# Page loads by pairs in the latent attention of a decoder layer, and low parts moved between GpSimd and VectorE

## Chip, cores and metric

The kernel runs on one core of one Trainium2 chip. The metric is the device time of one execution in microseconds; of several runs the median is given.

## The reference

One layer of a hybrid decoder is computed for 512 prompt tokens and for 8 sample sequences of 8 new tokens each: a first SwiGLU half-step, one input projection, a convolution branch, a latent attention branch, a gated merge, and a second SwiGLU half-step. All is float32. What matters here is the attention of the sample sequences over their paged cache of 2048 past tokens (16 pages of 128 tokens; a page holds 256 latent values and 32 rotary key values for each token):

```python
ckv = jnp.concatenate([cache_ckv_l[pages].reshape(past, KV_LORA), ckv_new], axis=0)
kpe = jnp.concatenate([cache_kpe_l[pages].reshape(past, QK_ROPE), kpe_new], axis=0)
k = build_keys(ckv, kpe, w_uk, k_head_norm)   # k_nope = w_uk c per head, joined with kpe, rms-normed per head
s = einsum('qhd,khd->hqk', q, k) * SCALE; s = where(mask, s, -inf)
p = softmax(s); o_lat = einsum('hqk,kc->qhc', p, ckv); o = einsum('qhc,chd->qhd', o_lat, w_uv)
```

## The kernel before

Five engines work side by side, each with its own written order, and they meet only at semaphores. SyncE issues the transfers. Float32 products are made from split operands: a value is rounded to a high part (ScalarE copies it to type fp32r), the low part is the rest (a subtraction), and a product is the sum of high x high, low x high and high x low.

Stages by time: first FFN to about 410 us, input projection and gates to about 600, prompt attention to about 705, sample sequences 705 to 1018, merge and output product to about 1170, second FFN to the end.

`sequences` runs the eight sample sequences s = 0 to 7 on each engine: s = 0 by itself, then a hardware loop with two sequences a turn for s = 1 to 4, then 5, 6 and 7 by themselves. SyncE has its own division: 0 and 1 written out, and a loop of three turns for 2 to 7. The buffer is b = s mod 2. A sequence has 16 pages, handled as 8 pairs (`pp`, PAIRS = 8) and as 4 groups of four (`g`). For one page t:

- The transposed latent page comes into `c_ring`, a ring of 8 pages (`load_ring`, L731). ScalarE makes the high part of a pair, `cT_hi` (`pages_hi`, L1300); VectorE the low part, `cT_lo` (`pages_lo`, L2466). Both have two buffers, for even and odd pairs.
- TensorE multiplies the page with keys and queries, 12 matmuls of 288 columns (L1861). ScalarE copies the scores out (L1345) and squares the keys (L1351), VectorE sums the squares for each head (L2646). TensorE waits for the squares of the page before last, ScalarE for the sums of the page before last.
- For every four pages `kpeT` (`load_kpe`, L742) gives the rotary part in one product (`kpe_scores`, L1825) behind page 3, 7, 11 and 15, and VectorE adds it (L2654).
- The page in its natural layout, `c_nat`, with two buffers of 16 pages (`load_rows`, L737), is needed a sequence later for the values. GpSimd squares its rotary part at the end of a sequence (`squares`, L964).

While s goes through its pages, the softmax and the values of r = s - 1 are woven in. The generators `soft_pe`, `soft_dve` and `soft_act` advance one step at each `next`. For r up to 5 (`stacked(s)`, s up to 6) the order is: VectorE forms `k_inv`, scales, takes the maxima and subtracts; ScalarE makes the exponentials at pages 8 and 9, twice: `p_two[.., 0, ..]` rounded and `s_buf` in full; GpSimd makes their low part in `p_two[.., 1, ..]` (`probabilities_low`, L945 and L947); ScalarE makes high parts `c_hi` of the pairs of `c_nat` (`pair_high`, L1332; four slots, EARLY_PAIRS = 4), GpSimd low parts in place (`split_pair`, L937); TensorE multiplies four pairs ahead of page 12 and four ahead of page 15 (L1781, L1782), and folds and transposes the result within page 15 (L1791, L1796). In sequence 7 the values of r = 6 are one plain product ahead of page 12 (L1802), which ends with `den_sum` from VectorE (L2540, L1808).

The page numbers lie in SBUF (`pages`). SyncE loads one into a register at L726, and each transfer takes its source address from such a register:

```python
def page_of(s, t):
    return sp.value_load(pages[0:1, ds(s * NP + t, 1)], min_val=0, max_val=pages_t.shape[0] - 1)
```

`load_pages` finds four page numbers for each group and issues with them four transfers to the ring, four to `kpeT` and four to `c_nat`. Behind the last sequence SyncE issues the first weights of the merge (`load_merge`, L618 and L619); ScalarE splits them within sequence 7 (`split_hi`, L461), behind pair 4 and ahead of the high part of pair 6.

Of the kernel before, what the change touches and what calls it, by code (L numbers as in the profile page):

```python
# [20 lines left out]
ds = bass.ds  # L21
# [72 lines left out]
def layer(nc, x_t, cols_in, pages_t, pages_in, pages_k, state_conv, page_table, w, const, out):  # L94

    ctx = ExitStack()
    with ctx:
# [213 lines left out]
        split_made = sem("split_made")  # L311
# [14 lines left out]
        nat_in = [[sem(f"nat_in{b}{g}") for g in range(NP // 4)] for b in range(2)]  # L326
        ring_in = [sem(f"ring_in{g}") for g in range(2)]
# [194 lines left out]
        SPLITS = PAIRS + 2  # L522
        HIGHS = PAIRS + 2
        LATE_AT = 11
# [9 lines left out]
        def pair_made(r, j):  # L534

            return r * SPLITS + (EARLY_PAIRS + 1 if j < EARLY_PAIRS else j + 3)
# [11 lines left out]
        PEB = 6  # L548

# [46 lines left out]
        def _(sp):  # L596
# [131 lines left out]
            def load_ring(g, found):  # L728

                for u, page in enumerate(found):  # L730
                    sp.dma_start(c_ring[:, (4 * g + u + RING // 2) % RING, :], pages_t[ds(page, 1), :, :].rearrange("a p c -> (a p) c"))\  # L731
                        .then_inc(ring_in[g % 2], 16)

            def load_rows(b, g, found):

                for u, page in enumerate(found):
                    sp.dma_start(c_nat[:, b, 4 * g + u, :], pages_in[ds(page, 1), :, :].rearrange("a p c -> (a p) c")).then_inc(nat_in[b][g], 16)  # L737

            def load_kpe(g, found):

                for u, page in enumerate(found):
                    sp.dma_start(kpeT[u * DR:(u + 1) * DR, g % 2, :], pages_k[ds(page, 1), :, :].rearrange("a d t -> (a d) t")).then_inc(kpe_in[g % 2], 16)  # L742

            def load_pages(s, b, used=None):

                for g in range(NP // 4):
                    found = [page_of(s, 4 * g + u) for u in range(4)]
                    sp.wait_ge(ct_lo, s * PAIRS + (2 * g - 2))
                    load_ring(g, found)
                    sp.wait_ge(pe_scored, s * (NP // 4) + (g - 1))  # L750
                    load_kpe(g, found)
                    if used is not None:
                        sp.wait_ge(pages_used, used + 2 * (g + 1))
                    load_rows(b, g, found)

            sp.wait_ge(rows_done, 2 * NT + PT_TILES)
            found = [page_of(0, u) for u in range(4)]
# [4 lines left out]
            for g in (1, 2):  # L762
                load_rows(0, g, [page_of(0, 4 * g + u) for u in range(4)])
# [2013 lines left out]
```

## Time and profile before

| | us |
|---|---|
| median of 3 runs (lowest, highest) | 1537.03 (1536.82, 1539.36) |
| the profiled execution | 1533.52 |
| its span in the trace | 1531.5 |
| TensorE busy | 1491.3 |
| VectorE busy | 1067.9 |
| ScalarE busy | 655.5 |
| GpSimd busy | 454.3 |

The span runs from the first to the last instruction of the trace. Busy times do not count register, branch and semaphore instructions or the issuing of transfers, so SyncE has no busy time in the page's table; its instructions show in its own timeline, as SPq. The chain of waits follows the last instruction back to whatever released each step.

### The profile page before, as it was taken

To read this page: it belongs to the slowest core of one execution; us is meant where nothing else is said; L and a number is where in the kernel's file an instruction comes from. 1 tells how busy PE (TensorE), PEld (TensorE's weight loads), DVE (VectorE), ACT (ScalarE), POOL (GpSimd) and SP (SyncE) were. 2 spreads that over 40 slices of the span, in tenths; PEclk is the share of its full clock that TensorE was granted. 3 is DMA by queue.
4 is the path that set the end of the run, shared out by engine and by line. 5 is a ranking of instruction groups with operands and counts; after the bars stand their busy time and mean duration, and the time that the engine had idled before them with its cause. 6 is when DMAs were issued, how large, how long until landed. Compare 5 with 4: busy or idle time off the path is not lost.

```text
span 1531.5 us, 31143 instructions
## 1 busy us (share of the span) xinstructions
PE 1491.3 (97%) x10771; PEld 1434.9 (94%) x10771; DVE 1067.9 (70%) x1738; ACT 655.5 (43%) x1215; POOL 454.3 (30%) x463
## 2 busy tenths in 40 slices
PE   8999999999999999999999888999999999999999
PEld 8999999999999999588888888888999999999999
DVE  7999898421269975865888788854759998985000
ACT  6444445322221242464666666642434444445111
POOL 4000002454465744320344333223551000005432
PEclk9999999999999999999999999999999999999999
DMA  6233234222333651003444443432222332332322
GB/s 176 70 103 103 82 97 116 78 83 75 82 83 100 83 116 47 13 4 99 129 127 129 124 125 111 128 106 72 83 83 56 109 97 85 106 92 81 91 77 82
DMA packets 245460, 141.69 MB, mean 93 GB/s; under 512 B 22705, under 2 KB 242290, under 8 KB 245362
## 3 DMA queue, kind: packets, MB, share of 16 engines
q1 hardware_dynamic: 244498, 139.97, 33.1%
q8 instruction: 54, 0.88, 0.2%
q10 hardware_dynamic: 864, 0.48, 0.1%
q14 instruction: 44, 0.36, 0.1%
HBM read 136.82 MB, written 3.58 MB: 92 GB/s over the span
## 4 chain that ended last, share of the span: by engine, by line
PE 52%; issue 24%; SPq 11%; POOL 7%; DVE 3%; ACT 1%; DMA 1%; POOLq 0%; DVEq 0%; ACTq 0%
PE ps L493 28%; PE ps L1522 14%; POOL w_lobuf L468 7%; SPq L726 3%; SPq L731 3%; SPq L742 3%; SPq L737 2%; PE ps L1861 2%; PE ps L1647 1%; PE ps L1701 1%; PE ps L1676 1%; PE ps L479 1%; PE ps L1691 1%; DMA w_rawbuf<-in_ffn_w_gu 1%; DVE cT_lo L2466 1%
## 5 line engine op out<-in xcount | busy, mean ns | idle before, releaser
L468 POOL TENSOR_TENSOR w_lobuf<-w_rawbuf,w_hibuf 128x256 fp32r<-128x256 f32 (+1 forms) x328 | 316.4, 996 | 801.4 <-ACT w_hibuf L461 801.3
L1522 PE MATMUL ps<-xs,w 128*128 128x288 f32 x3192 | 427.7, 296 | 0.8 <-DVE w L1984 0.8
L1522 PEld LDWEIGHTS ps<-xs,w 128*128 128x128 f32 x3192 | 426.8, 188 | 1.5 <-issue 1.5
L461 ACT ACTIVATE w_hibuf<-w_rawbuf 128x1024 fp32r<-128x1024 f32 (+1 forms) x89 | 104.4, 1173 | 353.3 <-PE ps L493 332.9
L2192 DVE SCALAR_TENSOR_TENSOR xT<-ps,xT 128x576 f32<-128x576 f32 x23 | 17.4, 756 | 202.4 <-PE ps L493 202.4
L1984 DVE TENSOR_TENSOR w<-w_raw,w 128x512 fp32r<-128x512 f32 x228 | 154.0, 690 | 0.3 <-ACT w L1029 0.2
L493 PE MATMUL ps<-a_hi,w_lobuf 128*128 128x288 f32 x682 | 147.5, 297 | 0.0
L493 PE MATMUL ps<-a_hi,w_hibuf 128*128 128x288 f32 x682 | 147.2, 296 | 0.0
L493 PE MATMUL ps<-x_hi,w_hibuf 128*128 128x288 f32 x656 | 142.2, 298 | 4.1 <-POOL w_lobuf L468 2.9
L493 PE MATMUL ps<-a_lo,w_hibuf 128*128 128x288 f32 x682 | 145.5, 294 | 0.0
L493 PE MATMUL ps<-x_lo,w_hibuf 128*128 128x288 f32 x656 | 140.8, 296 | 0.0
L493 PE MATMUL ps<-x_hi,w_lobuf 128*128 128x288 f32 x656 | 140.7, 296 | 0.0
L1029 ACT ACTIVATE w<-w_raw 128x512 fp32r<-128x512 f32 x228 | 132.2, 624 | 5.7 <-DVE w_raw L1978 2.4
L1861 PE MATMUL ps<-kq_hi,cT_hi 128*128 128x288 f32 x512 | 119.6, 316 | 14.7 <-DVE cT_lo L2466 9.3
L2215 DVE SCALAR_TENSOR_TENSOR y<-ext,cols,y 128x512 f32<-128x512 f32 x120 | 110.6, 922 | 4.1 <-DVE y L2215 1.4
L1861 PE MATMUL ps<-kq_hi,cT_lo 128*128 128x288 f32 x512 | 111.3, 299 | 0.0
L1861 PE MATMUL ps<-kq_lo,cT_hi 128*128 128x288 f32 x512 | 111.3, 299 | 0.0
L493 PEld LDWEIGHTS ps<-x_hi,w_hibuf 128*128 128x128 f32 x656 | 105.4, 188 | 5.8 <-POOL w_lobuf L468 4.1
L493 PEld LDWEIGHTS ps<-a_hi,w_hibuf 128*128 128x128 f32 x682 | 110.2, 189 | 0.0
L493 PEld LDWEIGHTS ps<-a_lo,w_hibuf 128*128 128x128 f32 x682 | 109.3, 188 | 0.0
L493 PEld LDWEIGHTS ps<-a_hi,w_lobuf 128*128 128x128 f32 x682 | 109.0, 188 | 0.0
L1861 PEld LDWEIGHTS ps<-kq_hi,cT_hi 128*128 128x128 f32 x512 | 84.1, 194 | 25.3 <-DVE cT_lo L2466 10.4
(335 smaller groups left out, 2602.6 us busy)
## 6 DMA issues: line engine op xcount, KB each, us to landing
w_raw<-in_ffn_w_gu SPq DMA_DIRECT2D x76, 256.0 KB, 2.9
up_rows<-in_ffn_w_gu SPq DMA_DIRECT2D x72, 256.0 KB, 3.2
c_nat<-in_pages_in SPq DMA_DIRECT2D x128, 144.0 KB, 2.2
c_ring<-in_pages_t SPq DMA_DIRECT2D x128, 128.0 KB, 2.1
w_rawbuf<-in_w_in SPq DMA_DIRECT2D x58, 256.0 KB, 3.2
w_rawbuf<-in_ffn_w_down SPq DMA_DIRECT2D x32, 384.0 KB, 4.0
w_rawbuf<-in_ffn_w_down SPq DMA_DIRECT2D x32, 320.0 KB, 3.4
w_rawbuf<-in_ffn_w_gu SPq DMA_DIRECT2D x24, 256.0 KB, 3.4
```

Source lines behind the costliest of these rows:

```text
L461: act.activation(w_hibuf[:, r % HIS, 0:size], w_rawbuf[:, r, 0:size], ACT.Copy).then_inc(w_hi_done, 1)
L468: ins = pool.tensor_tensor(w_lobuf[:, r, part], w_rawbuf[:, r, part], w_hibuf[:, r % HIS, part].bitcast(F32), ALU.subtract)
L493: mm = pe.matmul(ps[0:width, 2 * s + h, 0:HALF], a, b[:, k, h * HALF:(h + 1) * HALF], start=first and i == 0 and j == 0, stop=last and i = ...
L726: return sp.value_load(pages[0:1, ds(s * NP + t, 1)], min_val=0, max_val=pages_t.shape[0] - 1)
L731: sp.dma_start(c_ring[:, (4 * g + u + RING // 2) % RING, :], pages_t[ds(page, 1), :, :].rearrange("a p c -> (a p) c"))\
L737: sp.dma_start(c_nat[:, b, 4 * g + u, :], pages_in[ds(page, 1), :, :].rearrange("a p c -> (a p) c")).then_inc(nat_in[b][g], 16)
L742: sp.dma_start(kpeT[u * DR:(u + 1) * DR, g % 2, :], pages_k[ds(page, 1), :, :].rearrange("a d t -> (a d) t")).then_inc(kpe_in[g % 2], 16)
L1029: act.activation(w7[b][:, slot, 0, :], src, ACT.Copy).then_inc(w7_hi, 1)
L1522: mm = pe.matmul(ps[:, seven_bank(f, slot), 0:HALF], m, xs[:, slot, n, k, :], start=k == 0 and j == 0, stop=k == KH - 1 and j == 2)
L1861: mm = pe.matmul(ps[:, page_banks(t) + half, 0:KQ], a, m[:, half, cols], start=k == 0 and j == 0, stop=k == 1 and j == 2)
L1984: dve.tensor_tensor(w7[b][:, slot, 1, :], w7_raw[b][:, slot, 1, :], w7[b][:, slot, 0, :].bitcast(F32), ALU.subtract).then_inc(w7_lo, 1)
L2215: dve.scalar_tensor_tensor(dst, src, cw, dst, op0=ALU.mult, op1=ALU.add).then_inc(conv_p_step, 1)
```

## The change

- SyncE loads by pairs of pages. `load_pair` looks up two page numbers and issues two ring transfers, then looks up two page numbers for two transfers to `c_nat`: in the first half of a sequence those of the upper eight pages of the sequence before, in the second half those of its own lower eight. After each odd pair `load_kpe` looks up four numbers and issues four transfers to `kpeT`, two pairs or more behind the ring. The ring has one semaphore for each of its four pairs, and each `c_nat` buffer one for all of its 16 pages.
- `pages_lo` moves from VectorE to GpSimd, except in sequence 0.
- The low parts of the probabilities move from GpSimd to VectorE, ahead of pair 5, with a semaphore of their own, `p_low`.
- GpSimd's splits of the value pairs are interleaved with `pages_lo`.
- ScalarE makes the high parts of the last four value pairs from page 10 on, not 11. TensorE places four pairs of values ahead of page 11 and four within page 14; the fold comes ahead of the products of page 15. VectorE copies `o_lat` behind page 13 and inverts the denominator behind page 14.

```diff
-        split_made = sem("split_made")
+        split_made, p_low = sem("split_made"), sem("p_low")
...
-        nat_in = [[sem(f"nat_in{b}{g}") for g in range(NP // 4)] for b in range(2)]
-        ring_in = [sem(f"ring_in{g}") for g in range(2)]
+        nat_in = [sem(f"nat_in{b}") for b in range(2)]
+        ring_in = [sem(f"ring_in{j}") for j in range(RING // 2)]
...
-        SPLITS = PAIRS + 2
+        SPLITS = PAIRS
-        LATE_AT = 11
+        LATE_AT = 10
...
-            return r * SPLITS + (EARLY_PAIRS + 1 if j < EARLY_PAIRS else j + 3)
+            return r * SPLITS + (j + 1)
...
+        def pages_lo(eng, s, pp):
+            eng.wait_ge(ct_hi, s * PAIRS + (pp + 1))
+            eng.tensor_tensor(cT_lo[:, pp % 2, :], ring_pair(pp), cT_hi[:, pp % 2, :].bitcast(F32), ALU.subtract).then_inc(ct_lo, 1)
...
             def page_of(s, t):
                 return sp.value_load(pages[0:1, ds(s * NP + t, 1)], min_val=0, max_val=pages_t.shape[0] - 1)
-            def load_ring(g, found):
-                for u, page in enumerate(found):
-                    sp.dma_start(c_ring[:, (4 * g + u + RING // 2) % RING, :], pages_t[ds(page, 1), :, :].rearrange("a p c -> (a p) c"))\
-                        .then_inc(ring_in[g % 2], 16)
-            def load_rows(b, g, found):
-                for u, page in enumerate(found):
-                    sp.dma_start(c_nat[:, b, 4 * g + u, :], pages_in[ds(page, 1), :, :].rearrange("a p c -> (a p) c")).then_inc(nat_in[b][g], 16)
-            def load_kpe(g, found):
-                for u, page in enumerate(found):
-                    sp.dma_start(kpeT[u * DR:(u + 1) * DR, g % 2, :], pages_k[ds(page, 1), :, :].rearrange("a d t -> (a d) t")).then_inc(kpe_in[g % 2], 16)
-            def load_pages(s, b, used=None):
-                for g in range(NP // 4):
-                    found = [page_of(s, 4 * g + u) for u in range(4)]
-                    sp.wait_ge(ct_lo, s * PAIRS + (2 * g - 2))
-                    load_ring(g, found)
+            def found(s, t0, n):
+                return [page_of(s, t0 + u) for u in range(n)]
+            def load_ring(pp, two):
+                for u, page in enumerate(two):
+                    sp.dma_start(c_ring[:, (2 * pp + u + RING // 2) % RING, :], pages_t[ds(page, 1), :, :].rearrange("a p c -> (a p) c"))\
+                        .then_inc(ring_in[pp % (RING // 2)], 16)
+            def load_rows(b, pp, two):
+                for u, page in enumerate(two):
+                    sp.dma_start(c_nat[:, b, 2 * pp + u, :], pages_in[ds(page, 1), :, :].rearrange("a p c -> (a p) c")).then_inc(nat_in[b], 16)
+            def load_kpe(s, g):
+                four = found(s, 4 * g, 4)
+                if not (isinstance(s, int) and s == 0 and g < 2):
                     sp.wait_ge(pe_scored, s * (NP // 4) + (g - 1))
-                    load_kpe(g, found)
+                for u, page in enumerate(four):
+                    sp.dma_start(kpeT[u * DR:(u + 1) * DR, g % 2, :], pages_k[ds(page, 1), :, :].rearrange("a d t -> (a d) t"))\
+                        .then_inc(kpe_in[g % 2], 16)
+            def load_pair(s, b, pp, used=None):
+                two = found(s, 2 * pp, 2)
+                sp.wait_ge(ct_lo, s * PAIRS + (pp - 3))
+                load_ring(pp, two)
+                if pp >= PAIRS // 2:
+                    q = pp - PAIRS // 2
+                    two = found(s, 2 * q, 2)
                     if used is not None:
-                        sp.wait_ge(pages_used, used + 2 * (g + 1))
-                    load_rows(b, g, found)
+                        sp.wait_ge(pages_used, used + (q + 1))
+                    load_rows(b, q, two)
+                elif used is not None:
+                    q = pp + PAIRS // 2
+                    two = found(s - 1, 2 * q, 2)
+                    sp.wait_ge(pages_used, used + (q + 1 - PAIRS))
+                    load_rows(1 - b, q, two)
+                if pp % 2:
+                    load_kpe(s - 1 if pp == 1 else s, 3 if pp == 1 else (pp - 3) // 2)
             sp.wait_ge(rows_done, 2 * NT + PT_TILES)
-            found = [page_of(0, u) for u in range(4)]
-            load_ring(0, found)
-            load_kpe(0, found)
+            for pp in range(2):
+                load_ring(pp, found(0, 2 * pp, 2))
+            load_kpe(0, 0)
             sp.wait_ge(prep_q, 1)
-            load_rows(0, 0, found)
-            for g in (1, 2):
-                load_rows(0, g, [page_of(0, 4 * g + u) for u in range(4)])
+            for pp in range(6):
+                load_rows(0, pp, found(0, 2 * pp, 2))
             sp.wait_ge(prep_tr, 2)
             sp.wait_ge(uk_split, 1)
-            found = [page_of(0, 4 + u) for u in range(4)]
-            load_ring(1, found)
-            load_kpe(1, found)
-            load_rows(0, 3, [page_of(0, 12 + u) for u in range(4)])
-            for g in (2, 3):
-                found = [page_of(0, 4 * g + u) for u in range(4)]
-                sp.wait_ge(ct_lo, 2 * g - 2)
-                load_ring(g, found)
-                sp.wait_ge(pe_scored, g - 1)
-                load_kpe(g, found)
+            for pp in range(2, 4):
+                load_ring(pp, found(0, 2 * pp, 2))
+            load_kpe(0, 1)
+            for pp in range(6, PAIRS):
+                load_rows(0, pp, found(0, 2 * pp, 2))
+            for pp in range(4, PAIRS):
+                two = found(0, 2 * pp, 2)
+                sp.wait_ge(ct_lo, pp - 3)
+                load_ring(pp, two)
+            load_kpe(0, 2)
             sp.wait_ge(prep_mm, 2)
-            load_pages(1, 1)
+            for pp in range(PAIRS):
+                load_pair(1, 1, pp)
             with sp.Fori(1, NS // 2) as i:
                 for b in range(2):
-                    load_pages(i * 2 + b, b, i * (2 * PAIRS) + (EARLY_PAIRS + PAIRS * (b - 2)))
+                    for pp in range(PAIRS):
+                        load_pair(i * 2 + b, b, pp, i * (2 * PAIRS) + (EARLY_PAIRS + PAIRS * (b - 2)))
+            for q in range(PAIRS // 2, PAIRS):
+                sp.wait_ge(pages_used, EARLY_PAIRS + PAIRS * (NS - 3) + (q + 1))
+                load_rows(1, q, found(NS - 1, 2 * q, 2))
+            load_kpe(NS - 1, 3)
             sp.wait_ge(lat_mm, STACKED)
             for t in range(2):
...
                                    c_hi[j % EARLY_PAIRS][:, :, 0:KL].bitcast(F32), ALU.subtract)\
                     .then_inc(split_made, 1)
-            def probabilities_low(r, b, half):
-                t = slice(half * NP // 2, (half + 1) * NP // 2)
-                pool.wait_ge(p_done, exp_made(r, half))
-                ins = pool.tensor_tensor(p_two[:, t, 1, :], s_buf[:, b, t, :], p_two[:, t, 0, :].bitcast(F32), ALU.subtract)
-                if half:
-                    ins = pool.tensor_tensor(p_two[0:TS, NP, 1, :], s_buf[0:TS, b, NP, :], p_two[0:TS, NP, 0, :].bitcast(F32), ALU.subtract)
-                ins.then_inc(split_made, 1)
             def squares(s, b, uses, prev, nxt):
-                if prev and stacked(s):
-                    for j in range(EARLY_PAIRS):
-                        split_pair(s - 1, 1 - b, j)
-                    for half in range(2):
-                        probabilities_low(s - 1, 1 - b, half)
-                    for j in range(EARLY_PAIRS, PAIRS):
-                        split_pair(s - 1, 1 - b, j)
+                later = not (isinstance(s, int) and s == 0)
+                for pp in range(PAIRS):
+                    if later and pp < PAIRS - 1:
+                        pages_lo(pool, s, pp + 1)
+                    if prev and stacked(s):
+                        for j in ((), (), (0, 1), (2, 3), (), (4, 5), (6, 7), ())[pp]:
+                            split_pair(s - 1, 1 - b, j)
+                if not later:
+                    pool.wait_ge(ct_lo, PAIRS)
+                if nxt:
+                    pages_lo(pool, s, PAIRS)
                 if not nxt:
                     split_lo(pool, n_merge, n_merge % RAWS, KD * P)
-                for g in range(NP // 4):
-                    pool.wait_ge(nat_in[b][g], uses * 64)
+                pool.wait_ge(nat_in[b], uses * (16 * NP))
                 k = c_nat[:, b, :, KL:KL + DR]
                 pool.tensor_tensor(k, k, k, ALU.mult).then_inc(kpe_sq, 1)
...
-                act.wait_ge(ring_in[pp // 2 % 2], (s * 2 + (pp // 4 + 1)) * 64)
+                act.wait_ge(ring_in[pp % (RING // 2)], (s * 2 + (pp // 4 + 1)) * 32)
...
-                act.wait_ge(nat_in[b][j // 2], uses * 64)
+                act.wait_ge(nat_in[b], uses * (16 * NP))
...
+                    pe.wait_ge(p_low, r + 1)
...
                             pe.matmul(ps[:, page_banks(t) + part % 2, KQ:KQ + THIRD], ones[:, :], ln_acc[:, part * THIRD:(part + 1) * THIRD],
                                       start=True, stop=True)
                         if prev and stacked(s):
-                            for _ in range({12: 4, 15: 4}.get(t, 0)):
+                            for _ in range({11: 4, 15: 1}.get(t, 0)):
                                 next(soft)
                         cols = slice(SQ * b, SQ * b + KQ)
                         for k in range(2):
                             c = (2 * u + k) * P
                             hi, lo = cT_hi[:, pp % 2, c:c + P], cT_lo[:, pp % 2, c:c + P]
-                            if prev and k == 1 and t in ((7, 8, 15) if stacked(s) else (7, 8)):
+                            if prev and k == 1 and t in (7, 8):
                                 next(soft)
+                            if prev and stacked(s) and k == 1 and t == 14:
+                                for _ in range(EARLY_PAIRS):
+                                    next(soft)
                             for j, (a, m) in enumerate(((hi, kq_hi[:, k]), (lo, kq_hi[:, k]), (hi, kq_lo[k]))):
                                 if t == 0 and k == 0 and j == 2:
                                     pe.wait_ge(q_split, s + 1)
...
+                    yield
...
+            def probabilities_low(r, b):
+                for half in range(2):
+                    t = slice(half * NP // 2, (half + 1) * NP // 2)
+                    dve.wait_ge(p_done, exp_made(r, half))
+                    dve.tensor_tensor(p_two[:, t, 1, :], s_buf[:, b, t, :], p_two[:, t, 0, :].bitcast(F32), ALU.subtract)
+                dve.tensor_tensor(p_two[0:TS, NP, 1, :], s_buf[0:TS, b, NP, :], p_two[0:TS, NP, 0, :].bitcast(F32), ALU.subtract).then_inc(p_low, 1)
-                    if pp + 1 < NP // 2 or nxt:
-                        pages_lo(s, pp + 1)
+                    if isinstance(s, int) and s == 0 and pp + 1 < PAIRS:
+                        pages_lo(dve, s, pp + 1)
+                    if prev and stacked(s) and pp == 5:
+                        probabilities_low(s - 1, 1 - b)
...
-                        if prev and stacked(s) and t == NP - 2:
+                        if prev and stacked(s) and t in (NP - 3, NP - 2):
```

## Rows read from the trace of the kernel before

**Rows 1.** The page, part 1: busy time of the engines.

```profile
PE 1491.3 (97%) x10771; PEld 1434.9 (94%) x10771; DVE 1067.9 (70%) x1738; ACT 655.5 (43%) x1215; POOL 454.3 (30%) x463
```

**Rows 2.** Windows: length, busy PE, PEld, DVE, ACT, POOL, granted clock, DMA share, GB/s.

```profile
777.00:814.50 37.50, 34.25 (x246) 32.06 (x245) 31.25 (x51) 25.10 (x61) 15.12 (x12) 1.00 0.44 127
```

**Rows 3.** The chain of waits from 720 to 1030, shares by line.

```profile
by line: issue 20.9%; SPq L726 14.2%; SPq L731 13.3%; SPq L742 12.7%; SPq L737 11.9%; PE ps L1861 4.8%; PE ps L493 3.9%; DVE cT_lo L2466 2.6%; DVE page_ss L2646 2.0%; DMA w_rawbuf<-in_w_conv_out 1.6%; DMA c_ring<-in_pages_t 1.4%; ACT cT_hi 
```

**Rows 4.** Timeline of SyncE, one group: start, length, line, instructions.

```profile
777.40 2.61 SPq L731 DMA_DIRECT2D c_ring<-in_pages_t  x4
780.20 1.84 SPq L742 DMA_DIRECT2D kpeT<-in_pages_k  x4
782.29 1.92 SPq L737 DMA_DIRECT2D c_nat<-in_pages_in  x4
787.07 1.89 SPq L731 DMA_DIRECT2D c_ring<-in_pages_t  x4
```

**Rows 5.** Line L726 from 784.0 to 787.2: durations in ns, first and last start.

```profile
L726 SPq TENSOR_LOAD <-pages x4: 263/266/274, 784.4 to 786.3; - x4
```

**Rows 6.** Waits of SyncE's queue, 700 to 1060: total, times, longest.

```profile
SPq L742 <- PE ps L1825: 3.0, 2, 2.5
```

**Rows 7.** Timeline of SyncE: start and end of the loop, one loop end.

```profile
768.20 2.15 SPq L731 DMA_DIRECT2D c_ring<-in_pages_t  x4
...
837.64 1.92 SPq L737 DMA_DIRECT2D c_nat<-in_pages_in  x4
845.27 1.90 SPq L731 DMA_DIRECT2D c_ring<-in_pages_t  x4
...
992.96 2.69 SPq L737 DMA_DIRECT2D c_nat<-in_pages_in  x4
995.91 0.40 SPq L618 DMA_DIRECT2D w_rawbuf<-in_w_conv_out  x1
```

**Rows 8.** Timeline of SyncE, sequences 0 and 1.

```profile
705.76 2.25 SPq L731 DMA_DIRECT2D c_ring<-in_pages_t  x4
...
736.96 1.92 SPq L737 DMA_DIRECT2D c_nat<-in_pages_in  x4
741.29 1.88 SPq L731 DMA_DIRECT2D c_ring<-in_pages_t  x4
743.35 1.84 SPq L742 DMA_DIRECT2D kpeT<-in_pages_k  x4
```

**Rows 9.** Timelines of ScalarE, VectorE and TensorE behind SyncE's loop.

```profile
1001.21 1.06 ACT L461 ACTIVATE w_hibuf<-w_rawbuf 128x1024 fp32r<-128x1024 f32 x1 [6.06 <-DMA w_rawbuf<-in_w_conv_out]
...
1004.99 0.69 DVE L2466 TENSOR_TENSOR cT_lo<-c_ring,cT_hi 128x512 fp32r<-128x512 f32 x1 [9.79 <-ACT cT_hi L1300]
...
1007.56 0.37 PE L1808 MATMUL ps<-ones,den_sum 128*64 128x1 f32 x2 [3.11 <-DVE den_sum L2540]
```

**Rows 10.** Lines L2466, L937: ns min/median/max; the page, part 6.

```profile
L2466 DVE TENSOR_TENSOR cT_lo<-c_ring,cT_hi x64: 627/692/1523, 706.0 to 1010.0; 128x512 fp32r<-128x512 f32 x64
L937 POOL TENSOR_TENSOR c_lo<-c_nat,c_hi x48: 1187/1200/1732, 747.2 to 966.0; 128x512 fp32r<-128x512 f32 x48
c_nat<-in_pages_in SPq DMA_DIRECT2D x128, 144.0 KB, 2.2
```

**Rows 11.** Waits of TensorE, 700 to 1060: total us, times, longest.

```profile
PE ps L1861 <- DVE cT_lo L2466: 9.3, 17, 1.5
PE ps L1791 <- DVE o_lat L2533: 5.6, 5, 2.1
...
PE ps L1781 <- POOL p_two L947: 4.6, 4, 1.2
```

**Rows 12.** Windows around a stall of TensorE, columns as in rows 2.

```profile
850.00:852.00 2.00, 0.48 (x4) 0.48 (x5) 1.52 (x4) 0.41 (x1) 0.00 (x0) 1.00 0.65 175
...
854.00:856.00 2.00, 2.00 (x10) 1.91 (x9) 1.72 (x6) 0.07 (x1) 0.00 (x0) 0.50 0.27 81
856.00:858.00 2.00, 2.00 (x16) 2.00 (x16) 1.80 (x4) 0.71 (x2) 0.00 (x0) 0.98 0.63 193
```

More of the change, by code:

```diff
@@ L2461, in _ @@
             ins.then_inc(uk_split, 1)
-            def pages_lo(s, pp):
-                dve.wait_ge(ct_hi, s * PAIRS + (pp + 1))
-                dve.tensor_tensor(cT_lo[:, pp % 2, :], ring_pair(pp), cT_hi[:, pp % 2, :].bitcast(F32), ALU.subtract).then_inc(ct_lo, 1)
             dve.wait_ge(prep_tr, 3)
@@ L2483, in queries_lo @@
                 ins.then_inc(q_split, 1)
-            pages_lo(0, 0)
+            pages_lo(dve, 0, 0)
             dve.wait_ge(prep_lat, 2)
```

## The prediction

> **What bounds the kernel now.** I began with the page. TensorE is busy 97% of the span [rows 1], so at first sight only TensorE counts. The change, however, touches only the stretch in which eight sample sequences of 16 pages are worked off, about 705 to 1018 us, so I read that stretch alone. By windows, one sequence of the loop (777.0 to 814.5) takes 37.5 us, of which TensorE is busy 34.25 [rows 2]: there it is not full, and something else keeps nearly the same pace. The chain of waits over 720 to 1030 says what. Its largest shares are not TensorE's but SyncE's queue: L726 14.2%, L731 13.3%, L742 12.7%, L737 11.9%, together 52%, against 4.8% for the page products of L1861 [rows 3]. L726 is `page_of`, the load of one page number from SBUF into a register; the others issue transfers.
>
> SyncE's own timeline shows the pace. A group of four pages is 4 ring transfers, 4 of `kpeT`, 4 of `c_nat`, then a gap, then the next group's ring: 782.29 + 1.92 = 784.21 to 787.07, 2.86 us without a transfer [rows 4]. It is no wait: in it stand four register loads, started at 784.4 to 786.3, that is (786.3 - 784.4)/3 = 0.63 us apart, one after the other [rows 5]. Over the whole stretch the queue waited only 3.0 us for TensorE at L742 [rows 6]. So SyncE runs flat out: a group costs 1.89 + 0.25 + 1.84 + 0.25 + 1.92 + 2.86 = 9.01 us, a sequence 36.0. From 765.34 (768.20 less one gap of 2.86) to 995.65 (992.96 + 2.69) it takes 230.3 us for the 24 groups of sequences 2 to 7 [rows 7], 38.4 a sequence; 24 x 9.01 = 216.2 are regular. The other 14.1 are: at each of two loop ends a gap of 5.71 in place of 2.86 (837.64 + 1.92 = 839.56 to 845.27 [rows 7]; I take that for both), and 8.4 of transfers that issue more slowly (the four from 992.96 take 2.69, not 1.92).
>
> **The register loads, which decide it.** Before, `load_pages` finds four numbers and uses each three times: 16 loads a sequence. After, `load_pair` and `load_kpe` look numbers up anew for each use: 8 x 2 for the ring, 8 x 2 for the rows, 4 x 4 for `kpeT`, 48 a sequence. The 48 transfers stay 48. A load in the loop costs (2.86 - 0.25)/4 = 0.65 us; outside it, where the address is a constant, (2.41 - 0.18)/4 = 0.56 (gap 738.88 to 741.29, and 743.17 to 743.35 for a gap without loads [rows 8]). A batch of two transfers takes 0.85 (one takes 0.33, the next starts 0.52 later: (1.89 - 0.33)/3). A loop sequence is then:
> - 16 batches of two: 16 x 0.85 = 13.6
> - 16 gaps with two loads: 16 x (0.25 + 1.30) = 24.8
> - 4 batches of four and 4 gaps with four loads: 4 x (1.84 + 2.86) = 18.8
>
> Sum 57.2 us, against 36.0. Nothing hides it, since SyncE had no idle time to give.
>
> The Trainium skill ("DMA: Bandwidth & Descriptors", section "Latency and other measured facts") gives a floor of about 600 ns for such a load and says that unrolling by four amortises it. If four loads of a batch shared one cost, a batch of two would cost as much as one of four: 16 x 2.61 more a sequence, not 32 x 0.65. Here four batched loads start 0.63 us apart, so the trace shows the floor but no sharing.
>
> **The sum.** Everything is put on SyncE's clock in the profiled execution.
> - Start: it is released for the second ring group at 705.76 - 2.41 = 703.3 [rows 8]. From there the new order issues, for sequence 0, eight batches of two with two loads (0.85 + 1.30 = 2.15, 17.2) and two batches of four with four loads (1.84 + 2.41 = 4.25, 8.5): 729.0.
> - Sequence 1 (no upper rows of a predecessor): 12 x 2.15 + 4 x 4.25 = 42.8, to 771.8. The extra four loads of the first 12 row transfers fall before 703.3, in a wait, and cost nothing.
> - Sequences 2 to 7: 6 x 57.2 = 343.2, two loop ends 5.7, slow issues 8.4 x 57.2/36.0 = 13.3: to 1134.0.
> - New tail: rows of the last four pairs and the last `kpeT` group, 4 x 2.15 + 4.25 + 0.25 = 13.1: 1147.1.
>
> There SyncE issues the first merge weights (`load_merge`), which before it did at 995.91: +151.2. That issue passes the delay on. ScalarE waits for this transfer inside sequence 7 (idle until 1001.21), only then makes the next high part, VectorE's low part starts at 1004.99, its `den_sum` comes behind that, and TensorE, which waits for `den_sum`, goes on at 1007.56 [rows 9]. After the change `den_sum` no longer queues behind the low part, which GpSimd makes: TensorE can go on when the low part is there, at about 1004.99 + 1.2 = 1006.2 on the old clock. I take 2 us off. What follows (merge, output, second FFN) is untouched: +149.
>
> The profiled execution took 1533.5 us for a span of 1531.5; the median of the runs is 1537.0, 3.5 more. So the profiled one becomes 1682.7 and the median about 1686.
>
> **The other parts.** All lie in time that SyncE leaves, 57.2 less about 34 us of TensorE per sequence.
> - `pages_lo` moves to GpSimd. On VectorE it took a median 0.69 us (0.63 to 1.52); GpSimd's nearest row, the same shape, 1.20 (1.19 to 1.73) [rows 10]. In the chain of one pair that is +0.5 us of latency, once behind a transfer, not once a pair on SyncE. Per sequence GpSimd gets 8 x 1.2 to 1.7 more and loses the probabilities: some 22 of 57 us.
> - The low part of the probabilities goes to VectorE: two operations of the shape of L2466, 0.63 to 1.52 each, and a small one. Queued behind them are the page sums, which ScalarE needs two pages later; cover 20 us.
> - The placing of values at pages 11 and 14 and the fold at 15 issues the same matmuls. The waits that it can shorten are 4.6 (`p_two`) and 5.6 us (`o_lat`) over the whole stage [rows 11]; with SyncE late they are worth nothing, up to 10 us if it were not.
> - One `nat_in` counter for 16 pages. GpSimd's squares of sequence s, queued ahead of `pages_lo` for pair 1 of s+1, now wait for rows that SyncE issues in pair 3 of s+1; ScalarE's `pair_high` at page 2 waits for the same. So TensorE stands at page 2 of each sequence. SyncE itself needs that pair's low part only at pair 5, some 11 us behind those rows, and GpSimd has it about 2.2 (the transfer) + 2 x 1.2 = 4.6 us behind them [rows 10]. It costs nothing more as long as TensorE catches up in the 57 us.
>
> **Rivals.**
> - *TensorE at half clock is late too.* TensorE will idle for several us at a time. With 0.48 of 2 us busy (850 to 852) the granted clock was 0.50 from 854 to 856, the 1.2 GHz level, and 0.98 again by 856 to 858 under steady matmuls [rows 12]. If it stayed at half, 34 us of work would be 68, beyond 57.2: at worst 6 x 11 = 66 us more, 1752, and some 1715 for half of that. Against it: when TensorE is the late one it is busy, and the row shows it recover. The skill's "TensorE: Matmul & The Clock Gate", Part 1, has the same two levels and speaks against this change. Chance 0.11.
> - *Loads cost per batch, not each*: 16 x 2.61 - 21.2 = 20.6 more a sequence, 1810 and above. The spacing of the starts denies it. 0.03.
> - *Faster.* It needs the loads not to lie on the pace: SyncE's 57.2 without its 48 loads is 26.0, so to keep the present 38.4 with its 2.3 of slow issues and loop ends, a load would have to cost (38.4 - 2.3 - 26.0)/48 = 0.21 us. Then the change does what the waits invite, at most 9.3 + 5.6 + 4.6 = 19.5 us [rows 11], 1518 to 1533. One TENSOR_LOAD alone is 0.266 us, before its other register work [rows 5]. 0.04.
> - *No change*, SyncE's delay and those savings cancelling at a load near 0.25 us: 0.02.
>
> **How the numbers follow.** The forecast has 0.80, with its own range: 0.56 in place of 0.65 for a loop load takes 6 x 48 x 0.09 = 26 off; code that arrives more slowly at loop ends and a few us of TensorE a sequence add 20. That is 1660 to 1706. The range asked for reaches into the clock rival: 1664 to 1718. Within 0.2% (3 us, about what a measurement tells from nothing): 0.02; faster 0.04; slower 0.94.
>
> **What the new profile should show.** L726's successor has 48 register loads a sequence, 0.6 us apart; sequences are about 58 to 60 us from one `kpeT` product to the same of the next; the chain is mostly SyncE's queue; ScalarE waits for `c_ring` and `c_nat` transfers; TensorE's busy time is as before but its share falls to some 90% of the span, with a granted clock below 1 in places; after the merge weights all is as before, 150 us later. Wrong would be: loads that overlap, a queue that waits for `ct_lo` or TensorE, or a sequence above 62 us.

## The result, and the profile after

The changed kernel takes 1667.7 us (median of 4 runs, 1666.98 to 1671.18) against 1536.9 before: 8.55% slower, interval of the ratio 1.0833 to 1.0877, 130.8 us. The forecast was 1686, slower, range 1664 to 1718: the measured time lies 18 us below the forecast and 3.7 us above the low end of the range.

The page after, part 1, answers to [rows 1]:

```profile
PE 1533.8 (92%) x10771; PEld 1476.2 (88%) x10771; DVE 1048.0 (63%) x1700; ACT 657.8 (39%) x1215; POOL 507.4 (30%) x501
```

TensorE has the same 10771 matmuls and a smaller share, 92% for 97%, but its busy time rose by 42.5 us, from 1491.3 [rows 1]. The chain of waits from 730 to 1150, shares by line, answers to [rows 3]; L732 is now the register load, and L740, L746 and L754 issue ring, rows and `kpeT`. SyncE's four lines have 40.7% together; "issue" is time in which an engine waited for nothing that the profile shows:

```profile
by line: issue 40.6%; SPq L732 21.3%; SPq L746 6.9%; SPq L754 6.4%; SPq L740 6.1%; POOL cT_lo L553 5.6%; POOL c_lo L962 5.4%; PE ps L1884 4.0%; DMA w_rawbuf<-in_w_conv_out 0.8%; ACT L1406 0.3%; POOL c_nat L983 0.3%; ACT cT_hi L1319 0.3%; AC
```

SyncE's timeline for two pairs of pages, a quarter of a sequence, answers to [rows 4]:

```profile
851.23 0.90 SPq L740 DMA_DIRECT2D c_ring<-in_pages_t  x2
853.51 0.86 SPq L746 DMA_DIRECT2D c_nat<-in_pages_in  x2
855.87 0.86 SPq L740 DMA_DIRECT2D c_ring<-in_pages_t  x2
858.10 0.86 SPq L746 DMA_DIRECT2D c_nat<-in_pages_in  x2
861.46 1.84 SPq L754 DMA_DIRECT2D kpeT<-in_pages_k  x4
864.89 1.22 SPq L740 DMA_DIRECT2D c_ring<-in_pages_t  x2
```

From 851.23 to 864.89 are 13.66 us, 54.6 a sequence. Transfers take 5.32 of each 13.66; the gaps, 8.34, hold twelve register loads. Line L732, in the gap ahead of 861.46 and over the whole program (durations in ns, first and last start), answers to [rows 5]:

```profile
L732 SPq TENSOR_LOAD <-pages x4: 262/268/275, 859.0 to 860.7; - x4
...
L732 SPq FUSED_REGOPS  x501: 46/152/183, 649.4 to 1132.5; - x167
L732 SPq TENSOR_LOAD <-pages x384: 260/267/479, 648.9 to 1132.2; - x192
```

There are 384 loads in all, and within a batch each starts (860.7 - 859.0)/3 = 0.57 us behind the other. From 700 us to the end of its loop SyncE waited for nobody. The others waited for it; from the waits of 700 to 1150 (total us, times, longest):

```profile
POOL c_nat L983 <- DMA c_nat<-in_pages_in: 87.8, 6, 16.1
PE ps L1884 <- POOL cT_lo L553: 60.0, 14, 10.6
...
PE ps L1845 <- DMA kpeT<-in_pages_k: 38.6, 14, 6.0
```

This is the pattern foretold: GpSimd's squares stand in front of the next low parts and wait for late rows, and TensorE waits behind both. The windows show what TensorE's clock did (columns as in [rows 2]): the first 40 us, the whole stage, one sequence, and inside it 2 us without a matmul and 2 us shortly behind them:

```profile
0.00:40.00 40.00, 34.87 (x225) 34.45 (x226) 24.77 (x29) 25.11 (x40) 18.01 (x21) 0.87 0.57 168
705.00:1135.00 430.00, 316.32 (x1912) 294.10 (x1912) 225.20 (x356) 187.32 (x442) 147.68 (x123) 0.86 0.30 84
778.00:834.00 56.00, 39.70 (x243) 37.47 (x243) 28.84 (x47) 25.19 (x59) 22.27 (x18) 0.84 0.30 85
831.00:833.00 2.00, 0.00 (x0) 0.00 (x0) 1.84 (x3) 2.00 (x8) 0.00 (x0) 1.00 0.52 148
835.00:837.00 2.00, 2.00 (x12) 2.00 (x11) 1.36 (x3) 1.09 (x2) 0.60 (x1) 0.50 0.09 25
```

SyncE's timeline at the start and behind the end of its loop:

```profile
775.97 2.20 SPq L754 DMA_DIRECT2D kpeT<-in_pages_k  x4
...
1119.69 1.86 SPq L754 DMA_DIRECT2D kpeT<-in_pages_k  x4
1123.06 7.41 SPq L746 DMA_DIRECT2D c_nat<-in_pages_in  x8
1132.88 1.84 SPq L754 DMA_DIRECT2D kpeT<-in_pages_k  x4
1134.83 0.41 SPq L624 DMA_DIRECT2D w_rawbuf<-in_w_conv_out  x1
```

SyncE reaches the merge weights at 1134.83, 138.9 us later than at 995.91 [rows 7]; from there to the end of the span it is 1669.2 - 1134.83 = 534.4 us, before 1531.5 - 995.91 = 535.6.

### The profile page after: what moved, and what is told of

Its sections match the earlier page's. It is cut to its first block, busy times and chain, and to the rows that moved or that the text cites. A ratio compares the mean times of both kernels' runs of the same rounds, so it can differ in the third digit from the quotient of the medians.

```text
span 1669.2 us, 31936 instructions
## 1 busy us (share of the span) xinstructions
PE 1533.8 (92%) x10771; PEld 1476.2 (88%) x10771; DVE 1048.0 (63%) x1700; ACT 657.8 (39%) x1215; POOL 507.4 (30%) x501
## 4 chain that ended last, share of the span: by engine, by line
PE 48%; issue 29%; SPq 11%; POOL 9%; DMA 1%; ACT 1%; DVE 1%; POOLq 0%; ACTq 0%
PE ps L493 26%; PE ps L1541 12%; POOL w_lobuf L468 6%; SPq L732 5%; PE ps L1884 2%; SPq L746 2%; SPq L754 2%; SPq L740 2%; POOL cT_lo L553 1%; POOL c_lo L962 1%; PE ps L1666 1%; PE ps L1720 1%; PE ps L1695 1%; DMA w_rawbuf<-in_ffn_w_gu 1%; PE ps L479 1%
## 5 line engine op out<-in xcount | busy, mean ns | idle before, releaser
L1884 PE MATMUL ps<-kq_hi,cT_hi 128*128 128x288 f32 x512 | 132.7, 344 | 60.6 <-POOL cT_lo L553 60.0
L1884 PEld LDWEIGHTS ps<-kq_hi,cT_hi 128*128 128x128 f32 x512 | 95.2, 216 | 68.3 <-POOL cT_lo L553 35.7
L2675 DVE TENSOR_REDUCE page_ss<-sq 128x8 f32<-128x512 f32 x128 | 84.3, 676 | 99.6 <-ACT sq L1370 99.4
L553 POOL TENSOR_TENSOR cT_lo<-c_ring,cT_hi 128x512 fp32r<-128x512 f32 x56 | 76.7, 1370 | 167.7 <-ACT cT_hi L1319 167.7
L1884 PE MATMUL ps<-kq_hi,cT_lo 128*128 128x288 f32 x512 | 120.1, 319 | 0.0
L1884 PE MATMUL ps<-kq_lo,cT_hi 128*128 128x288 f32 x512 | 118.5, 315 | 0.0
```

The costliest lines, as they stand in the source:

```text
L553: eng.tensor_tensor(cT_lo[:, pp % 2, :], ring_pair(pp), cT_hi[:, pp % 2, :].bitcast(F32), ALU.subtract).then_inc(ct_lo, 1)
L1884: mm = pe.matmul(ps[:, page_banks(t) + half, 0:KQ], a, m[:, half, cols], start=k == 0 and j == 0, stop=k == 1 and j == 2)
L2675: dve.tensor_reduce(page_ss[:, t, :], sq[:, u, 0:H * DN].rearrange("p (h d) -> p h d", d=DN), AX, ALU.add).then_inc(page_red, 1)
```

## Experiments

Times are medians. Each ratio is to the kernel before, run beside the experiment on the same chip, with its interval in brackets. Where medians of two experiments lie close, the ratios decide, since not all ran on one chip.

**1. The loads alone.** The kernel before, 8 more loads a group, unused.

```diff
                     found = [page_of(s, 4 * g + u) for u in range(4)]
+                    for u in range(8):
+                        page_of(s, 4 * g + u % 4)
                     sp.wait_ge(ct_lo, s * PAIRS + (2 * g - 2))
```

> The kernel before with nothing changed but 32 more register loads of page numbers in each of sequences 1 to 7 (8 more a group, their results unused), so 48 a sequence as in the changed kernel. Theory (SyncE's register loads set the pace): 7 x 32 x 0.56 to 0.65 us, so 125 to 145 us more than before, 1660 to 1682, nearly all of the change's loss. Rival (the loss comes from GpSimd's new place in the chain, from the one counter for 16 pages or from TensorE's clock falling by itself): no more than 10 us above before, 1547 at most, since none of these is here.

Measured: 1654.96 us, 1.0775 [1.0748, 1.0801], 118 us more. That is 118 of the change's 131 us with no engine but SyncE altered, and the rival's 10 us are far off. The theory holds; its size was missed, 118 where at least 125 were expected. The chain, 720 to 1040:

```profile
by line: SPq L726 38.3%; issue 24.9%; SPq L731 11.9%; SPq L742 11.7%; SPq L737 11.2%; PE ps L1863 0.6%; PE ps L1763 0.4%; PE ps L1764 0.3%; SPq L755 0.2%; SPq L750 0.2%; SPq L752 0.2%; PE ps L1827 0.1%; SPq L780 0.1%
```

**2. A smaller dose.** The same with `for u in range(2)`: 2 more loads a group.

> The kernel before with 8 more register loads in each of sequences 1 to 7 (2 more a group, unused), 24 in all. It asks how much room SyncE had in the kernel before. If it had none: 7 x 8 x 0.58 = 32 us more, 1569. If it had the room that the run with 32 more loads leaves open (7 x 32 x 0.58 = 130 us of loads cost only 118): 20 us more, 1557. If TensorE or VectorE were the real pace: under 5 us.

Measured: 1562.72, 1.0173 [1.0149, 1.0198], 26.7 us more, between the two cases of 20 and 32. For 56 loads that is 0.48 us each, for the 224 of experiment 1 it is 0.53. At 0.57 us a load they should cost 31.9 and 127.7 us, so 5 to 10 us are missing. They are not idle time of SyncE that the loads filled: its waits at L742 were 3.0 us before and are 2.2 here and 3.7 in experiment 1. Some 3 to 4 us are transfers that issue faster: from the first to the last ring group of the loop their lengths add up to 135.5 us before, 132.2 here and 131.7 in experiment 1. The rest was not traced, and each measured difference is uncertain by about 4 us.

**3. The change without its loads.** `load_pair` gives way to the loop of before; the rest of the change stays (main lines of the edit).

```diff
-            def load_pair(s, b, pp, used=None):
...
+            def load_pages(s, b, used=None):
+                for g in range(NP // 4):
+                    four = found(s, 4 * g, 4)
+                    sp.wait_ge(ct_lo, s * PAIRS + (2 * g - 2))
+                    for h in range(2):
+                        load_ring(2 * g + h, four[2 * h:2 * h + 2])
+                    sp.wait_ge(pe_scored, s * (NP // 4) + (g - 1))
+                    put_kpe(g, four)
...
+                    for h in range(2):
+                        load_rows(b, 2 * g + h, four[2 * h:2 * h + 2])
```

> The changed kernel with SyncE's stream of before put back: four page numbers found once for a group, used for ring, kpeT and rows; all else of the change stays (GpSimd makes the low parts of pages, VectorE those of probabilities, values at pages 11 and 14, one counter for each buffer of rows). Theory: 1525 to 1545, since the loads are back to 16 a sequence; the rest of the change is then worth -10 to +8 us. Rival (the rest of the change costs most): above 1600.

Measured: 1555.18, 1.0115 [1.009, 1.014]. Of the 131 us 112 are gone, so the rival falls, but 18 stay, more than the 8 that I allowed. TensorE's waits, 700 to 1060, and the timelines of ScalarE, GpSimd, VectorE and TensorE at page 11 of one sequence show where:

```profile
PE ps L1876 <- POOL cT_lo L553: 12.3, 14, 2.3
PE ps L1793 <- ACT sq L1362: 12.1, 3, 4.3
PE ps L1793 <- DVE p_two L2620: 10.9, 3, 4.1
```

```profile
808.03 0.25 ACT L1335 ACTIVATE s_buf<-s_buf 64x64 f32<-64x64 f32 x1
```

```profile
808.87 1.26 POOL L553 TENSOR_TENSOR cT_lo<-c_ring,cT_hi 128x512 fp32r<-128x512 f32 x1 [4.43 <-ACT cT_hi L1311]
```

```profile
807.59 1.41 DVE L2619 TENSOR_TENSOR p_two<-s_buf,p_two 128x512 fp32r<-128x512 f32 x2
808.91 1.29 DVE L2620 TENSOR_TENSOR p_two<-s_buf,p_two 64x64 fp32r<-64x64 f32 x1
```

```profile
810.31 0.36 PE L1793 MATMUL ps<-c_hi,p_two 128*128 128x258 f32 x1 [3.90 <-ACT sq L1362]
```

L1793 is the first product of values. It starts 0.11 us behind the last subtraction for the probabilities (808.91 + 1.29 = 810.20), so both rows of its waits, 23.0 us over six sequences, are that wait; ScalarE's squares, which the one row names, had ended before. TensorE waits from 810.31 - 3.90 = 806.41. ScalarE's last exponential ends at 808.03 + 0.25 = 808.28: page 11 is too early for the exponentials, and that is 1.87 us of the 3.90.

The rest is VectorE, and a part of it comes from the low parts of pages that now run on GpSimd. The last subtraction is small, 64x64, and takes 1.29 us. It starts 0.04 us behind GpSimd's `pages_lo` (808.87) and ends 0.07 us behind it; this is so in all six sequences, and in the changed kernel too. In `b_plow_nb` (experiment 9), where VectorE makes these low parts itself, the same subtraction takes 0.21 us in all six:

```profile
802.02 0.21 DVE L2599 TENSOR_TENSOR p_two<-s_buf,p_two 64x64 fp32r<-64x64 f32 x1
```

So VectorE's small subtraction was not done before GpSimd's was. That is 1.08 us a sequence on TensorE's path, by estimate 6 x 1.08 = 6.5 of the 18 us.

**4. Values at page 12.** Experiment 3 with

```diff
-        LATE_AT = 10
+        LATE_AT = 11
...
-                            for _ in range({11: 4, 15: 1}.get(t, 0)):
+                            for _ in range({12: 4, 15: 1}.get(t, 0)):
```

> The changed kernel with SyncE's stream of before, and the first four pairs of values placed ahead of page 12 again, not 11 (and ScalarE's late high parts from page 11). Theory A (the 18 us that this kernel keeps over before come from TensorE's wait at page 11 for the probabilities, 23 us over six sequences): the probabilities are ready some 4 us after page 10 ends and one page more covers 1.6 us of each wait, so at least 9 us less than 1555, 1538 to 1546. Theory B (the slower low parts of pages on GpSimd cost it): no change, 1552 to 1556.

Measured: 1535.96, 1.0002 [0.9987, 1.0017]: 19.2 us back by the medians, 17 by the ratios, all that the rest of the change cost, and 2 us more than the range of theory A. B as it was put, a cost that stays whatever the placing, falls. GpSimd's share in the wait at page 11 (experiment 3) is part of what the later placing covers: in five of the six sequences the small subtraction still takes 1.30 us here. TensorE's wait for `p_two`:

```profile
PE ps L1793 <- DVE p_two L2620: 5.4, 5, 1.2
```

**5. The same edit in the changed kernel.** Only `{12: 4, 15: 1}` and `LATE_AT = 11`.

> The changed kernel as it is, with SyncE's 48 loads a sequence, and only the first four pairs of values placed ahead of page 12 again. In the kernel with SyncE's stream of before this gave back 19 us. Theory (SyncE sets the pace, TensorE's waits lie in its shadow, as the prediction costed them): within 3 us of the changed kernel's 1668. Rival (TensorE's wait at page 11 adds to SyncE's time): 1645 to 1655.

Measured: 1668.81, 1.0861 [1.0841, 1.088]; the changed kernel 1667.7, 1.0855. What was worth 17 to 19 us beside the old stream is worth nothing here: it lies in SyncE's shadow, that is, in time that TensorE would otherwise spend waiting for SyncE. TensorE's waits from 770 to 1140 in the changed kernel and then in this one:

```profile
PE ps L1884 <- POOL cT_lo L553: 49.4, 13, 8.8
PE ps L1845 <- DMA kpeT<-in_pages_k: 31.1, 12, 4.5
PE ps L1801 <- ACT sq L1370: 11.6, 3, 4.3
PE ps L1801 <- DVE p_two L2628: 10.1, 3, 3.7
```

```profile
PE ps L1845 <- DMA kpeT<-in_pages_k: 51.0, 18, 4.4
PE ps L1884 <- POOL cT_lo L553: 47.0, 7, 8.6
```

The 21.7 us at L1801 are gone, and 19.9 us more are spent waiting for `kpeT`, which SyncE issues.

**6. The order by pairs with numbers kept.** The changed kernel; a dictionary keeps page numbers in registers through the unrolled code, 20 loads a sequence in the loop.

```diff
+            kept = {}
...
+                for u in range(n):
+                    if (at, t0 + u) not in kept:
+                        kept[at, t0 + u] = page_of(s, t0 + u)
+                return [kept[at, t0 + u] for u in range(n)]
```

> The changed kernel with its own order of transfers, but page numbers found once and kept in registers where the unrolled code allows it: 20 loads a sequence in the loop, not 48. Theory: 28 loads fewer in each of six sequences at 0.58 us is 97 us less, some 15 more in sequences 0, 1 and the tail: 1550 to 1575. Rival (the order by pairs or the late rows and kpeT cost by themselves): above 1620. If register loads were overlapped or cheap: as the changed kernel, 1668.

Measured: 1567.21, 1.0192 [1.0167, 1.0217], as expected: 100 us back with the order of transfers as it is in the changed kernel. How the 30 us that stay over the kernel before divide was not taken apart in this run.

**7. Shorter loads in the changed kernel.** The range check is left out of `page_of`.

```diff
-                return sp.value_load(pages[0:1, ds(s * NP + t, 1)], min_val=0, max_val=pages_t.shape[0] - 1)
+                return sp.value_load(pages[0:1, ds(s * NP + t, 1)])
```

> The changed kernel as it is, but each page number loaded without its range check. A load then costs 0.26 us less (in the kernel before the gap with four loads shrank from 2.86 to 1.81 us). Theory: 6 x 48 x 0.26 = 75 us less in the loop and some 17 us less around it (68 loads), 92 in all, as long as SyncE stays the pace: 1576 to 1592. Rival (the count of instructions or of batches costs, not the loads' own length): 1640 or more.

Measured: 1579.31, 1.0278 [1.0261, 1.0295]: 88.4 us less, within the expected range. The number of loads and batches is the same; what stands behind each load is shorter. So the loss is the time that a lookup takes, times their number, and not a price for each batch.

**8. The same in the kernel before.**

> The kernel before with the range check of each page number left out (the check's register instructions and the assert go, the load stays). Theory (SyncE was already the pace of before): each load loses 0.15 to 0.25 us, 16 a sequence, six to seven sequences: 14 to 25 us less, 1512 to 1523, or less where TensorE's own 34 us a sequence becomes the limit. Rival (TensorE and VectorE were the pace of before, SyncE only just kept up): within 3 us of before.

Measured: 1527.93, 0.9936 [0.9912, 0.9961], 9.1 us less, a real gain but under the expected 14. The timeline of SyncE, its waits from 700 to 1060 and the chain of waits from 720 to 1040:

```profile
828.81 1.92 SPq L737 DMA_DIRECT2D c_nat<-in_pages_in  x4
832.55 1.89 SPq L731 DMA_DIRECT2D c_ring<-in_pages_t  x4
```

```profile
SPq L742 <- PE ps L1825: 30.9, 8, 6.3
```

```profile
by line: PE ps L1861 18.8%; issue 17.0%; DVE cT_lo L2466 8.9%; DVE page_ss L2646 8.8%; PE ps L493 5.3%; ACT cT_hi L1300 2.5%; PE ps L1802 2.2%; DVE s_buf L2515 2.1%; DVE y L2215 2.1%; ACT sq L1351 2.0%; ACT s_buf L1322 1.9%; PE ps L1825 1.9
```

The gap fell to 832.55 - 830.73 = 1.82 us from 2.86, 0.26 a load, and SyncE now waits 30.9 us for TensorE's scores where it waited 3.0 [rows 6]. It has stopped being the pace: the chain of waits now names TensorE and VectorE first. The 96 loads of the loop became 25 us shorter and the kernel only 9. So lengthening SyncE's stream costs at once (2), and shortening it brings little; that a further shortening would bring nothing is likely, but was not run.

**9. Toward a faster kernel.** These are three combinations without the range check. The first is the kernel of experiment 4 without it.

> The same, and the range check of page numbers left out as well. If VectorE's load was what held the kernel without the check at 1528, taking the low parts of pages off it should gain further: 1515 to 1526. If GpSimd's longer chain from transfer to matmul costs more than it frees: 1528 to 1540.

Measured: 1530.44, 0.9968 [0.9958, 0.9979], no faster than experiment 8. To take the low parts of pages off VectorE gained nothing.

> The kernel before without the range check, and of the change only the low parts of the probabilities moved from GpSimd to VectorE (values at pages 12 and 15 as before). TensorE's wait for them at page 12 was 4.6 us in all and VectorE's two subtractions take 0.7 us each against GpSimd's 1.3: 2 to 6 us less than 1528 where VectorE has room, 0 to 5 more where it has none. That tells which engine should have that part.

Its edit moves `probabilities_low` to VectorE ahead of pair 5, with the semaphore `p_low`, in experiment 8's kernel. Measured: 1524.61, 0.993 [0.9902, 0.9957]. The interval covers that of experiment 8 nearly whole, so whether VectorE or GpSimd has this part is not told apart.

> The change with its own order of transfers, with its three costs taken away: page numbers kept in registers (20 loads a sequence), no range check, values at page 12. SyncE then needs some 54.6 - 28 x 0.58 - 20 x 0.26 = 33 us a sequence, less than TensorE. If the order by pairs gives TensorE its pages earlier: 1515 to 1528. If it gives nothing that the stream by fours lacks: 1528 to 1540, with the best of the kernels still the one at 1524.6.

Measured: 1534.06, 0.9993 [0.998, 1.0007]. With every cost found here removed, the order by pairs is only as fast as the kernel before, which keeps its range check, and behind the stream by fours in the same state (`a_stream_v12_nb`, 0.9968, with 16 loads a sequence for 20), so it gives TensorE nothing.

**10. GpSimd takes two of eight pairs.** `b_plow_nb` with the low parts of pairs 2 and 3 on GpSimd:

```diff
+        def on_pool(s, pp):
+            return pp in (2, 3) and not (isinstance(s, int) and s == 0)
```

> The fastest so far (the kernel before without the range check, low parts of the probabilities on VectorE, 1524.6), and GpSimd makes the low parts of pairs 2 and 3 of each sequence, where TensorE waited most for VectorE, which is then busy with scaling and maxima; the other six pairs stay on VectorE. TensorE's waits for low parts there were 9.1 us in all. If they are VectorE's queue: 3 to 8 us less, 1517 to 1522. If GpSimd's 1.2 us and its own splits cost as much: 1524 to 1530.

Measured: 1523.02, 0.9924 [0.9908, 0.994], between the two cases that were expected, the lowest median of all and not told apart from `b_plow_nb`. TensorE's waits for low parts, 9.1 us at VectorE there, moved to GpSimd and did not shrink:

```profile
PE ps L1867 <- POOL cT_lo L559: 9.6, 7, 1.7
```

It is 12.5 us under the kernel before. Of these 9.1 come with the range check left out (8); the interval does not tell the rest from nothing.

## Why the prediction was right, and what was mis-sized

- *SyncE's register loads set the pace.* Right. 48 loads a sequence, one behind the other, no wait in SyncE's loop; 118 us come from the loads alone (1), and the loss shrinks with their number (3, 6) and with the time that each takes (7).
- *The loop load at 0.65 us.* This is the term that was too large. The gaps are 8.34 us in each 13.66, against 9.06 forecast, with 0.1 us more of transfers: 54.6 us a sequence, not 57.2, which is 15.4 us over six. By the prediction's own measure a load cost (8.34 - 5 x 0.25)/12 = 0.59 us. In the loop of before nearly every load carried one more register operation than its check needs: 233 for 140 loads in all, 93 more, for the 96 loads of the loop. After, there are 501 for 384, 117 more, although 288 loads lie in the loop. So the price of before did not carry over, and that of a load outside the loop, 0.56, was the better one. Why the compiled code needs fewer of these operations was not looked into.
- *Slow issues and loop ends.* SyncE's loop took from 778.17 to 1121.55, 343.4 us; less 24 x 13.66 = 327.8 it leaves 15.6, of which two loop ends have 2 x 2.6. Slow issues are thus 10.4, where I scaled them to 13.3, and loop ends 5.2, not 5.7. The loop in all: 343.4 against 362.2.
- *Start, sequence 1, tail.* It took 70.7 us from the release (708.80 less the 1.29 of two loads, 707.5) to 778.17, against 68.5; the tail 13.3 against 13.1.
- *The rest untouched.* 534.4 against 535.6: 1.2 less, forecast 2.
- *How these meet the measured time.* 151.2 - 18.8 + 2.2 + 0.2 - 1.2 = 133.6. The profiled execution shows 137.7, because it was already 4.2 late at 707.5. It began with TensorE's clock at 0.87 over the first 40 us, where that of before had 1.00, and SyncE's first transfer to `w_raw` behind 50 us starts at 57.68, before at 53.34. At 1671.2 it is 3.5 above its median. That of before was 3.4 below its own. 137.7 - 3.5 - 3.4 = 130.8, the measured difference.
- *`pages_lo`, values at page 11, one counter of rows: hidden.* Right for the changed kernel, shown for the values by 5 and for the others only together, by SyncE's loop without a wait. But the prediction said that without SyncE's cover the new placing would be worth up to 10 us; it costs 17 to 19 (3, 4). I took the waits of before as what an earlier placing could save and did not ask when its input is ready. In the kernel before, at page 12, the last exponentials release GpSimd at 800.00 and TensorE waits only from 802.10 - 1.15 = 800.95; a page, by estimate 37.5/16 = 2.3 us, earlier it would have met ScalarE still at work. Nor did the prediction see that `pages_lo` on GpSimd holds up VectorE's subtraction. From the timelines of GpSimd and TensorE in the kernel before:

```profile
800.00 1.28 POOL L945 TENSOR_TENSOR p_two<-s_buf,p_two 128x512 fp32r<-128x512 f32 x1 [0.64 <-ACT s_buf L1324]
```

```profile
802.10 0.38 PE L1781 MATMUL ps<-c_hi,p_two 128*128 128x258 f32 x1 [1.15 <-POOL p_two L947]
```

- *TensorE's clock.* It did fall, to 0.84 in one sequence and 0.86 over the stage: from 831 to 833 no matmul ran, and from 835 to 837 the granted clock was 0.50, the 1.2 GHz level. But TensorE caught up each time: SyncE waited for nobody, so the rival of 0.11 stayed a rival. The Trainium skill ("TensorE: Matmul & The Clock Gate", Part 1) leads one to expect the lower clock in such gaps; the trace agrees, with 0.50 behind the one at 831, and in this stage it cost nothing.
- *TensorE's busy time as before.* Wrong: it is 42.5 us more, 33.6 of them in this stage (316.3 from 705 to 1135, 282.7 from 705 to 1018 before), because the same matmuls last longer at the lower clock (512 of the page products, high by high, take 344 ns each at L1884, at L1861 before 316). Being off SyncE's path, this did not touch the sum.
- *Loads paid by the batch.* Excluded: starts 0.57 us apart within a batch, and 0.48 to 0.53 us for each further load in 1 and 2. But the prediction was also wrong to say that the trace shows a floor of about 0.6 us for such a load. The load itself takes 0.27 us, and without the check one starts about 0.57 - 0.26 = 0.31 us behind the other (7, 8).
- *The range.* 1664 lies above the prediction's own case of a load at 0.56, 1660. With a load at 0.59 the time came out 3.7 us above that low end; the mechanism was sure, the place in the range less so.
- *The faster and the unchanged case* needed a load of 0.21 to 0.25 us. Without its check, at about 0.57 - 0.26 = 0.31 us, the changed kernel is at 1579: still slower, as that bound has it.

## What to carry to other kernels

An engine that only issues transfers has no busy time on the page. Read its timeline for gaps that hold no wait, and price what stands in them before adding any. A value that is looked up again is paid on that engine's pace: here 32 more lookups a sequence cost 118 of the 131 us. A cost in another engine's shadow is still a cost: test it with the cover gone before calling the part free. Before a product is placed earlier, ask when its last input is ready, and not only how long it waits now.

## What the runs showed of the hardware

- A register load from SBUF takes 0.26 to 0.27 us, but with its range check it starts 0.57 us behind the last; the check is nearly half of that (0.26 us a load by the gaps of experiment 8).
- Register loads whose results nobody uses are executed all the same (1 and 2: 364 and 196 TENSOR_LOADs, for 140 before).
- At each turn of SyncE's loop 2.6 us (after) to 3.2 us (before) more than usual pass in which nothing is issued; why was not tested.
- A 64x64 subtraction on VectorE took 0.21 us by itself and 1.29 to 1.31 us when GpSimd had begun a 128x512 subtraction 0.04 us earlier; it ended with GpSimd's (3, 4 and the changed kernel).
- Behind 2 us in which TensorE ran no matmul (831 to 833) the granted clock was 0.50, the 1.2 GHz level (835 to 837 in the changed kernel); with SyncE as the pace this cost no time.
